# A two-layer decoder trunk on one core: the last expert job's first down slots ahead of a scatter, the final norm by halves, and three smaller moves

## What is computed

```python
x = x + mlstm_mixer(rmsnorm(x, norm_mix[0]), ...)      # layer 0
x = x + swiglu_dense(rmsnorm(x, norm_ffn[0]), ...)     # 1024 -> 2816 -> 1024
shared = nsa_shared_kv(rmsnorm(x, norm_kv), ...)       # layer 1
x = x + nsa_mixer(rmsnorm(x, norm_mix[1]), shared, ...)
x = x + moe_swiglu(rmsnorm(x, norm_ffn[1]), ...)       # top 2 of 8 experts
return rmsnorm(x, norm_final)
# one expert e of moe_swiglu, for the tokens that chose it:
act = silu(t @ w_gu[e][:, :3584]) * (t @ w_gu[e][:, 3584:]) * gate[:, e]
y  += act @ w_down[e]
```

## Time and profile before

| | us |
|---|---|
| median of 3 runs | 1437.31 (1434.43 to 1438.07) |
| the profiled execution | 1439.59 |
| its span | 1437.8 |
| TensorE busy | 1391.2 (97%) |
| VectorE busy | 1184.5 (82%) |
| ScalarE busy | 1022.9 (71%) |
| GpSimd busy | 43.8 (3%) |
| data moved | 431.68 MB, mean 300 GB/s |

### The profile page before, as it was taken

One profiled execution on the slowest core, in us unless ns is written; L12 is line 12 of the kernel. 1 busy time (PEld: TensorE's weight loads), 2 busy tenths in 40 slices (PEclk: granted clock), 3 DMA queues, 4 the chain that ended last, 5 costly groups with the idle time before them and its releaser, 6 DMA issues.

```text
span 1437.8 us, 19005 instructions
## 1 busy us (share of the span) xinstructions
PE 1391.2 (97%) x6962; PEld 1142.7 (79%) x6962; DVE 1184.5 (82%) x1091; ACT 1022.9 (71%) x1066; POOL 43.8 (3%) x98
## 2 busy tenths in 40 slices
PE   7999999999999989999999999999999999999996
PEld 7987888888974578788888878888878888878774
DVE  6846654547768679899999999999999999999997
ACT  5546644435567747788888788887878887887875
POOL 7000000001000010000000000000000000000000
PEclk9999999999999989999999999999999999999999
DMA  7543555554630129899999999999999999999985
GB/s 307 177 162 131 192 189 178 176 203 147 235 118 1 39 94 350 326 394 416 407 399 402 399 391 402 411 395 403 398 388 398 408 409 395 391 401 398 415 353 214
DMA packets 59707, 431.68 MB, mean 300 GB/s; under 512 B 6624, under 2 KB 6624, under 8 KB 7520
## 3 DMA queue, kind: packets, MB, share of 16 engines
q1 hardware_dynamic: 59472, 429.95, 76.8%
q10 hardware_dynamic: 144, 0.52, 0.1%
HBM read 429.40 MB, written 1.05 MB: 299 GB/s over the span
## 4 chain that ended last, share of the span: by engine, by line
PE 89%; DVE 4%; DMA 3%; ACT 2%; issue 1%; POOL 0%; SPq 0%; DVEq 0%; POOLq 0%; ACTq 0%
PE bank L1475 19%; PE bank L1477 19%; PE bank L1476 19%; PE bank L1946 6%; PE bank L1947 6%; PE bank L2008 3%; PE bank L1965 3%; PE bank L1966 3%; DMA raw<-in_moe 3%; PE bank L1823 2%; PE bank L1849 2%; DVE w_lo L1352 1%; PE bank L1917 1%; PE bank L1833 1%; PE bank L1995 1%
## 5 line engine op out<-in xcount | busy, mean ns | idle before, releaser
L1352 DVE TENSOR_TENSOR w_lo<-raw,w_hi 128x2048 fp32r<-128x2048 f32 x332 | 750.6, 2289 | 46.7 <-ACT w_hi L748 44.0
L748 ACT ACTIVATE w_hi<-raw 128x2048 fp32r<-128x2048 f32 x332 | 632.9, 1919 | 137.5 <-DMA raw<-in_moe 58.7
L1475 PE MATMUL bank<-w_hi,ht_hi 128*128 128x512 f32 (+1 forms) x768 | 299.3, 390 | 0.9 <-DVE ht_lo L885 0.9
L1477 PE MATMUL bank<-w_hi,ht_lo 128*128 128x512 f32 (+1 forms) x768 | 296.2, 386 | 0.0
L1476 PE MATMUL bank<-w_lo,ht_hi 128*128 128x512 f32 (+1 forms) x768 | 295.9, 385 | 0.0
L853 DVE TENSOR_TENSOR w_lo<-raw,w_hi 128x2048 fp32r<-128x2048 f32 x73 | 166.6, 2290 | 109.7 <-ACT w_hi L433 109.6
L433 ACT ACTIVATE w_hi<-raw 128x2048 fp32r<-128x2048 f32 x74 | 141.4, 1918 | 96.4 <-PE bank L1477 92.8
L1946 PE MATMUL bank<-w_hi,ht_hi 128*128 128x512 f32 x448 | 177.5, 396 | 1.4 <-DVE w_lo L1352 1.4
L1947 PE MATMUL bank<-w_lo,ht_hi 128*128 128x512 f32 x448 | 174.8, 390 | 0.0
L1475 PEld LDWEIGHTS bank<-w_hi,ht_hi 128*128 128x128 f32 x768 | 144.4, 188 | 29.6 <-issue 1.4
L1477 PEld LDWEIGHTS bank<-w_hi,ht_lo 128*128 128x128 f32 x768 | 144.3, 188 | 29.4
(11 more groups left out here) (328 smaller groups left out, 1671.1 us busy)
## 6 DMA issues: line engine op xcount, KB each, us to landing
raw<-in_moe SPq DMA_DIRECT2D x336, 1024.0 KB, 7.8
raw<-in_wts SPq DMA_DIRECT2D x71, 1024.0 KB, 4.9
xs<-in_x SPq DMA_DIRECT2D x2, 512.0 KB, 4.0
out<-xn SPq DMA_DIRECT2D x2, 512.0 KB, 2.6
pk<-in_packed SPq DMA_DIRECT2D x1, 517.0 KB, 5.9
g1b<-in_norm_ffn ACTq DMA_DIRECT2D x1, 512.0 KB, 3.8
gfb<-in_norm_final SPq DMA_DIRECT2D x1, 512.0 KB, 12.0
```

What stands on the lines that cost most here:

```text
L748: a(w_hi[:, n % SPLIT, :], raw[:, n % RAW, :], ACT.Copy).then_inc(s_hi, 1)
L1352: v.tensor_tensor(w_lo[:, n % RAW, :], raw[:, n % RAW, :], w_hi[:, n % SPLIT, :].bitcast(F32), ALU.subtract).then_inc(s_lo, 1)
L1475: mm(out_, sh, mh, start=first, stop=False)
L1477: return mm(out_, sl, mh, start=False, stop=last)
```

## The change

It has these parts; the sketch of the diff below keeps what the prediction speaks of.

1. **Down slots ahead of the scatter.** In the last paired phase (`following == "last"`) TensorE does slots L+0 and L+1 right after its own work, before the scatter of the large job, into banks 0 and 1. The rest of the last job's down slots go to banks 0 and 1 too, and `y_hi`, `y_lo` read them there. In both last phases the scatter uses banks 6, 7, 5 and 2.
2. **The last slot by halves.** Of slot L+13 only the first 1024 columns are split. Its second half (the product's second k block) is done by two plain float32 matmuls from `raw` and `avt`, which need no split, then four matmuls do the first half.
3. **The final norm by 512 columns.** Squares, stores and scaling go by halves of a tile. GpSimd adds EPS to the first half's mean square, adds the second, and takes the power, where it scaled and took the power before.
4. **`hg_lo` of tile 0 on VectorE.** It stands between `residual(.., (3,))` and the second `tile_low`; ScalarE's `gained_high(0)` moves ahead of the two squares.
5. **Slot 0's load ahead of `pk`**, and ScalarE's split of slot 0 ahead of the wait for `pk`.

```diff
@@ SyncE
-        sp.dma_start(pk[:], packed).then_inc(s_pk, 16)
         for n in range(N0):
             load(n, wts[n, :, :])
+            if n == 0:
+                sp.dma_start(pk[:], packed).then_inc(s_pk, 16)
...
-        for t in range(NT):
-            sp.wait_ge(s_fin, t + 1)
-            sp.dma_start(out[0, t * P:(t + 1) * P, :], xn[:, t, :]).then_inc(s_out, 16)
+        for n in range(4):
+            t, half = divmod(n, 2)
+            w = slice(half * 512, half * 512 + 512)
+            sp.wait_ge(s_fin, n + 1)
+            sp.dma_start(out[0, t * P:(t + 1) * P, w], xn[:, t, w]).then_inc(s_out, 16)
@@ GpSimd
-        pool.wait_ge(s_hgh, 1)
-        g.tensor_tensor(hg_lo[:, 0, :], xn[:, 0, :], hg_hi[:, 0, :].bitcast(F32), ALU.subtract).then_inc(s_hgl, 1)
-        norm_rstd(4)
+        for t in range(NT):
+            mean, inv = stats[:, 16 + t:17 + t], stats[:, 18 + t:19 + t]
+            pool.wait_ge(s_sq, 4 * NT + 2 * t + 1)
+            step(g.tensor_scalar(mean, stats[:, 56 + 2 * t:57 + 2 * t], EPS, None, ALU.add))
+            pool.wait_ge(s_sq, 4 * NT + 2 * t + 2)
+            step(g.tensor_tensor(mean, mean, stats[:, 57 + 2 * t:58 + 2 * t], ALU.add))
+            g.tensor_tensor(inv, mean, consts[:, 0:1], ALU.pow).then_inc(s_rstd, 1)
@@ ScalarE
         squares(0)
+        split_to(0)
         act.wait_ge(s_pk, 16)
-        split_to(0)
...
+        gained_high(0)
         act.wait_ge(s_xu, 11)
...
-        gained_high(0)
         gained_high(1)
...
+            if up is None:
+                n = first + length - 1
+                act.wait_ge(landed[n % RAW], i * (16 * 2 * JOB_SLOTS // RAW) + 16 * (n // RAW + 1))
+                act.wait_ge(s_used, i * (2 * JOB_SLOTS) + (n - SPLIT + 1))
+                a(w_hi[:, n % SPLIT, 0:1024], raw[:, n % RAW, 0:1024], ACT.Copy).then_inc(s_hi, 1)
@@ VectorE
         residual(2, (0, 1, 2, 7), N0 - 1, (3,))
+        gained_low(0)
         tile_low(5, 1, 6, (4, 5, 2, 7), (2, 3))
...
-                for n, bank in enumerate((6, 7, 1, 5)):
+                for n, bank in enumerate(scatter_banks(gather is None)):
...
         for t in range(NT):
+            inv = stats[:, 18 + t:19 + t]
             dve.wait_ge(s_rstd, 4 * NT + t + 1)
+            for half in range(2):
+                w = slice(half * 512, half * 512 + 512)
+                v.scalar_tensor_tensor(xn[:, t, w], xs[:, t, w], inv, gfb[:, w], ALU.mult, ALU.mult).then_inc(s_fin, 1)
@@ TensorE
+        def last_down(i, n):
+            pe.wait_ge(landed[n % RAW], i * (16 * 2 * JOB_SLOTS // RAW) + 16 * (n // RAW + 1))
+            pe.wait_ge(s_bact, i * 7 + 7)
+            for half in range(2):
+                mm(B[half][0:CAP_B, :], avt[:, 0, 3 * CAP_B:4 * CAP_B], raw[:, n % RAW, 1024 + half * 512:1536 + half * 512],
+                   start=False, stop=False)
+            pe.wait_ge(s_lo, i * (2 * JOB_SLOTS) + (n + 1))
+            pe.wait_ge(s_blo, i * 7 + 7)
+            block = slice(26 * P, 27 * P)
+            for half in range(2):
+                w = slice(half * 512, half * 512 + 512)
+                mm(B[half][:, :], at_b[:, block], weights(w_hi, n, 1024)[:, 0, w], start=False, stop=False)
+                ins = mm(B[half][:, :], at_b[:, block], weights(w_lo, n, 1024)[:, 0, w], start=False, stop=True)
+                if half == 0:
+                    ins.then_inc(s_y, 1)
+            ins.then_inc(s_used, 1)
...
+            if following == "last":
+                pe.wait_ge(s_bg, i * 7 + 7)
+                pe.wait_ge(s_bu, i * 7 + 7)
+                for d in range(2):
+                    down_part(i, first + length + down_slot(d, False), d, 1, 0)
+            elif following is not None:
...
-            for n, b in enumerate((6, 7, 1, 5)):
+            for n, b in enumerate(scatter_banks(gather_at is None)):
...
-        phase(rounds, N0 + UP_SLOTS, 1, 0, 0, None, None, None)
+        phase(rounds, N0 + UP_SLOTS, 1, 0, 0, None, None, "last")
```

More of the change, by code:

```diff
@@ L268, in down_slot, with scatter_banks @@
         return 3 * d + 2 if paired else d
+    def scatter_banks(late):
+        return (6, 7, 5, 2) if late else (6, 7, 1, 5)
     block = ctx.enter_context(nc.Block())
@@ L769, in phase @@
                 if up is None:
-                    split(down_slot(m, paired) + AHEAD)
+                    split(min(down_slot(m, paired) + AHEAD, length - 2))
                     if m == 0:
@@ L821, in phase @@
                         used(length - 1)
-                    a(y_hi[:, h * 512:(h + 1) * 512], B[2 + h][:, :], ACT.Copy, scale=gcol[:, down:down + 1]).then_inc(s_yh, 1)
+                    a(y_hi[:, h * 512:(h + 1) * 512], B[(0 if up is None else 2) + h][:, :], ACT.Copy, scale=gcol[:, down:down + 1]).then_inc(s_yh, 1)
             if up == 1:
                 silu_b(6, 0)
-            split(length - 1 + TURN)
+            if up is not None:
+                split(length - 1 + TURN)
         phase(0, N0, 0, 0, None, 3, 1)
@@ L839, in _ @@
         phase(rounds, N0 + UP_SLOTS + JOB_SLOTS, None, 0, 1, None, None)
-        squares(4, rounds * 8 + 16, junk)
+        for n in range(4):
+            t, half = divmod(n, 2)
+            w = slice(half * 512, half * 512 + 512)
+            act.wait_ge(s_xu, rounds * 8 + (17 + n))
+            a(junk[:, t, w], xs[:, t, w], ACT.Square, scale=D ** -0.5,
+              accum_out=stats[:, 56 + 2 * t + half:57 + 2 * t + half]).then_inc(s_sq, 1)
     @block.vector
@@ L1428, in phase @@
                         gathered_low((m - gather - 5) // 2, B[7], gather_job * 2, 1 - up)
-            split(length - 1 + AHEAD)
+            if up is None:
+                n = first + length - 1
+                dve.wait_ge(s_hi, i * (2 * JOB_SLOTS) + (n + 1))
+                v.tensor_tensor(w_lo[:, n % RAW, 0:1024], raw[:, n % RAW, 0:1024], w_hi[:, n % SPLIT, 0:1024].bitcast(F32),
+                                ALU.subtract).then_inc(s_lo, 1)
+            else:
+                split(length - 1 + AHEAD)
             if down is not None:
@@ L1444, in phase @@
                     v.tensor_tensor(xv, xv, B[bank][:, :], ALU.add).then_inc(s_xu, 1)
-                    split(length - 1 + min(AHEAD + n, TURN))
-            split(length - 1 + TURN)
+                    if up is not None:
+                        split(length - 1 + min(AHEAD + n, TURN))
+            if up is not None:
+                split(length - 1 + TURN)
         phase(0, N0, 0, 0, None, 3, 1)
@@ L2029, in phase @@
                         turned(6, 0)
-                if down is not None:
+                if up is None and m == DOWN_SLOTS - 1:
+                    last_down(i, first + down_slot(m, paired))
+                elif up is None and m >= 2:
+                    down_part(i, first + down_slot(m, paired), m, down, 0)
+                elif paired:
                     down_part(i, first + down_slot(m, paired), m, down)
```

19 lines of the change are left out of this document (9 added, 10 removed).

## The result

| | before | after |
|---|---|---|
| median | 1436.94 us (1434.43 to 1438.07, 4 runs) | 1427.83 us (1427.04 to 1430.38, 4 runs) |
| profiled execution, its span | 1439.59, 1437.8 | 1427.04, 1425.3 |

The account below looks back on a forecast made before the run. TensorE was taken to set the pace from the start to the border of the last two jobs; 1.4 + 1.15 + 5.1 + 0.5 + 0.5 = 8.65 off the median 1437.31 gave 1428.7 us, range 1425.5 to 1432.5.

Parts of the forecast that it names:

- What bounds the kernel: From 556 to 1387 us TensorE sets the pace; whatever starts this stretch earlier moves all of it.
- rival 4: Before 540 us another engine ends last somewhere, so an early gain is absorbed: 1430.1 to 1431.2 us, chance 0.06.
- Slot 0 ahead of `pk`: At the start, slot 0 lands earlier without 517 KB ahead of it: gain 1.4 us, first product at 12.5.
- Rival 1: At the start TensorE's clock stays up behind the shorter stall: 1.5 us more, 1427.2 us, chance 0.15.
- `hg_lo` on VectorE: At the router, L1211 is no longer slowed by GpSimd: 1.15 us gained at L1909, bounds nothing to 1.3.
- L+0 and L+1 ahead of the scatter: At the last two jobs' border, L+4's split starts 2.7 us earlier and nine run back to back: gain 5.1.
- The last slot by halves: At the end, L+13's half split and two float32 matmuls at 0.43 each: gain 0.5 us, bounds 0.2 to 0.7.
- Final norm: At the end, half-tile squares, scaling and stores: gain 0.5 us, bounds -0.3 to 0.9.
- rival 2: Transfers set the tail, so the end comes 1.5 or 3 us later: 1430.2 to 1431.7 us, chance 0.14.
- The long stretch: From 540 to 1387 us: the prediction is wrong if this stretch changes its length by over 2 us.

Follow-up runs that it names:

- load_first: The kernel before with only slot 0's load moved ahead of `pk` and its split ahead of the wait for `pk`: median 1435.00 us against 1437.11, ratio 0.9987.
- after_again: The changed kernel run once more, unchanged, for its spread: median 1428.70 us, ratio 0.9931.
- two_halves: The changed kernel with L+13 split in two halves, four matmuls behind each, no plain float32 matmul: median 1428.85 us, ratio 0.9947.
- full_last: The changed kernel with slot L+13 split whole again and done with eight matmuls: median 1427.58 us, ratio 0.9938.
- router_warm: two_halves plus ten dummy transposes behind the router's logits and five behind its counts: median 1427.80 us, ratio 0.9930.
- border_only: The kernel before with only L+0 and L+1 moved ahead of the scatter: median 1432.72 us against 1436.70, ratio 0.9974.
- hglo_only: The kernel before with only `hg_lo` of tile 0 on VectorE and `gained_high(0)` ahead of the two squares: 1433.94 us in one run.
- one_ahead: As border_only, but with L+0 alone ahead of the scatter: 1433.94 us in one run.
- norm_only: The kernel before with only the final norm and stores by 512 columns: 1437.57 us in one run.

## Why the prediction was right, and where it wasn't

1. **What bounds the kernel** held: in the pair the start's 2.96 reached the router but for 0.38, and the router's gain reached the gather, so rival 4 (absorbed) falls there. (What load_first lost again on the way goes with its extra half clock.) TensorE's largest wait for VectorE from 540 to 1385 us is as small as in the earlier trace rows:

```profile
PE bank L1509 <- DVE w_lo L1376: 2.3, 4, 0.7
```

2. **Slot 0 ahead of `pk`, 1.4**: 1.36 over thirteen profiles, 1.54 in the pair.
3. **Rival 1, the clock at the start** (1.5, given a chance of 0.15): it came true in the change's own profile (1.42) and failed in after_again (7.53, which is 0.28 worse than before). Two things had to come together, and I had weighed one. The clock must rise by about the end of the transposes: it did, at 10.3 to 12.1, in seven of thirteen profiles, among them the one of before, whose last two transposes lie 0.11 and not 0.21 apart ("barely warmed" fits), and in the other six not until 16.3 to 19.5. And it must hold through the stall: of the seven it held where the stall was 0.83 to 2.08 or filled (five), and fell where it was 2.40 and 3.13 (two). The change shortens the stall and so helps with the second only. Four of six profiles with the early slot 0 were fast, so a chance of about two in three on 1.4 would have been nearer.
4. **`hg_lo` on VectorE, 1.15**: 1.01 alone, 1.18 in the pair. The row went from 1.46 to 0.17 and TensorE's wait from 3.79 to 2.51 as worked out. The Trainium skill (SBUF — State Buffer, "Who interferes with whom") agrees with the trace: beside GpSimd's subtraction the row took 1.46, without it 0.17. The gather behind it was 0.71 shorter in the pair, but 0.28 and 0.36 longer in two_halves and full_last; over all, it is 8.73 on average with part 4 (six) and 8.59 without (seven), so it is no gain of the edit. From the square through the gather part 4 leaves 0.9 on average (22.96 for 23.88): 1.7 in the change and router_warm, 0.5 in the other four. In the short ones the last gather matmuls are already back at full pace.
5. **L+0 and L+1 ahead of the scatter, 5.1**: measured 5.17 to the end of L+12's split. The steps held too, counted from the copy of `av`, which came 7.07 earlier: L+4's split forecast for 1396.4 - 7.07 = 1389.33, seen at 1389.33; L+12's end forecast for 1409.3, seen at 1409.23. What I had not weighed is how the 5.4 of border_only divide: 3.6 for the stall and its clock, 1.8 for slots and loads, and one slot would have done. And the border was costly in the profile of before: with half clock for 3.4 us and not 6.8 the same border took 2 us less, so that the mean gain over the profiles is 4.5, not 5.1.
6. **The last slot by halves, +0.5: this step failed.** It costs 0.95 against the full split (full_last) and 0.92 in the pair. I priced two plain float32 matmuls at 0.43 each from the earlier trace rows, where I read "x2" as two instructions. Each call is two rows, so the 1.02 of that group was one call. In L2010 two calls give four rows and take 1.86, not 0.86. That single misreading is 1.0 of the 1.1 to 1.4 by which the step was off (5.31 instead of 4.2 from L+12's split end; my bound for a slow matmul, 0.6, was too near as well). Some 0.3 more went between the second `y_hi` and the last update (4.57 for 4.26), which I didn't trace further. two_halves, which does the same halves without plain float32, reaches 4.21.
7. **Final norm, 0.5**: 0.98 alone, 1.18 in the pair. The smaller store gave 0.6, I had put 0.15; that is the mis-sized term. The chain, forecast at 0.35, gave 0.36 alone and 0.57 in the pair. GpSimd did meet VectorE's halves as feared, 0.96 for 0.56.
8. **The transfers (rival 2)** came close: ScalarE waited about 0.6 for a load ahead of the last splits, but VectorE, a slot behind, never did.

```profile
1406.05 1.06 ACT L829 ACTIVATE w_hi<-raw 128x1024 fp32r<-128x1024 f32 x1 [0.60 <-DMA raw<-in_moe]
```

9. **The long stretch.** I had said I would be wrong if it changed its length by over 2 us. In the pair it is 2.60 shorter. Over thirteen profiles it lies between 844.6 and 848.3; the profile of before holds the longest, and that execution was 2.65 above its median. The kernels with parts 4 and 5 together (five) average 845.3, the others (eight) 846.6, with ranges that overlap (844.6 to 845.9 and 844.8 to 848.3). By part 4 alone they part better: 844.6 to 845.9 with it (six, mean 845.2), 845.9 to 848.3 without (seven, mean 846.9). In the pair 0.8 of the 2.60 is one stall of TensorE, which only before and load_first have at that size:

```profile
PE bank L2071 <- DVE y_lo L1434: 0.8, 1, 0.8
```

That line is of before. The grouping was made after the fact. hglo_only, with part 4 alone, has 844.8, but one profile of it doesn't settle the matter, so whether part 4 gains 1 to 2 us in this stretch or chance does is open.

By the terms of the pair the change is 1.4 + 1.1 + 5.2 - 0.9 + 1.1 = 7.9, and the start's clock adds 1.4 in some executions. By means over the profiles it is 1.4 for slot 0, 1.1 for the start's clock, 0.9 for the router and gather, 4.5 for the border, 0.95 lost with the last slot and 1.1 for the norm: 8.0 together, without the open 1 to 2 of the long stretch. Measured are 9.1, with an interval of 7.0 to 11.4 (0.9951 and 0.9921 of 1437). So the forecast of 8.65 came close with errors that partly cancelled, which is luck: 1.4 too much for the last slot and 0.6 too much for the border, against 0.6 too little for the norm and the start's clock, which was left out of the sum.

The best form that the experiments point to is the change with two_halves' last slot (router_warm and two_halves have it): 1427.80 and 1428.85 against 1427.83 and 1428.70 for the change. The segment gains 1.3 each time; the run times, taken in different sessions, can't tell them apart.

## What to carry to other kernels

Before a row's duration prices an instruction, divide the number of rows by the number of calls in the code: one call can be two rows. Where TensorE stalls long enough to lose its clock, ask what it could do meanwhile: here reordered real work gave 4.5 us on average (5.4 against one profile), and dummy work in the same place 2.7 (3.6). And one profiled pair is a poor judge of small terms: the two spans differ by 12.5 us and the medians by 9.1, and which segments held the excess showed only when they were read in thirteen profiles.

## What the runs showed of the hardware that I had not expected

- A plain float32 matmul of 512 columns took 0.93 us at full clock and shows as two rows; the rounded form takes 0.234.
- The column of the clock reads 1.00 ahead of the first entry of the trace's list, also where TensorE is at half clock. That list begins at 10.3 to 12.1 in seven profiles and at 16.3 to 19.5 in six (after_again, router_warm, border_only, one_ahead, hglo_only, norm_only), and in these six the matmuls ahead of it lie 0.21 apart, not 0.12. Count the matmuls of a window beside its clock.
- hglo_only shows it behind the long stall, 15 matmuls in 3 us, where full clock gives 27:

```profile
14.00:17.00 3.00, 3.00 (x15) 3.00 (x16) 3.00 (x7) 3.00 (x5) 2.41 (x7) 1.00 1.01 426
```

- The same code had the clock up before its first product in one profile and not in another (the change 11.03, after_again 16.27), after transposes that look alike (16 of them, 0.21 apart, from 7.46).
- 15 transposes in the router's waits did not bring the clock back (matmuls stayed 0.43 apart), 20 ahead of the scatter, right behind full-rate work, kept it.
- Taking 517 KB out from ahead of a 1 MB load brought it in 1.36 earlier, at 0.39 MB/us (0.53 MB by 1.36), between the 0.281 and 0.43 MB/us of the earlier trace rows.
